# Two units of products on unscaled x, with the inverse root applied behind them, and x in eight column pieces

## The reference

```python
def _hybrid_layer(h, norm_w, w_in, ...):
    u = _rmsnorm(h, norm_w)                 # h * rsqrt(mean(h*h) + 1e-6) * norm_w
    proj = jnp.matmul(u, w_in)              # 2048 -> 22576 columns, then split
    (ml_q, ml_k, ml_v, ml_o, ml_z, ml_i, ml_f,
     dn_qkv, dn_z, dn_b, dn_a, gate_a, gate_b) = jnp.split(proj, idx, axis=-1)
    i_pre = _softcap(ml_i + ml_i_bias)
    logf  = log_sigmoid(_softcap(ml_f + ml_f_bias))
    qkv = _causal_conv_silu(dn_qkv, dn_conv_w)          # 4 taps over time
    ...
    beta = sigmoid(dn_b)
    g = -exp(dn_a_log) * softplus(dn_a + dn_dt_bias)
```

## Time and profile before

| | us |
|---|---|
| runs | 1913.67, 1914.96, 1916.21; median 1914.96 |
| span of the profiled execution | 1913.3 |
| TensorE, VectorE, ScalarE, POOL busy | 1895.3, 1398.8, 947.8, 344.2 |

### The profile page before, as it was taken

The page is one execution under the profiler, slowest core; times in us unless marked ns, Lnnn a source line. Parts: engine busy times, 40 slices in busy tenths (PEclk is TensorE's granted clock), DMA queues, the critical chain, the costliest instruction groups (busy, mean ns, idle before and its releaser), DMA issues.

```text
span 1913.3 us, 27611 instructions
## 1 busy us (share of the span) xinstructions
PE 1895.3 (99%) x10948; PEld 1638.9 (86%) x10948; DVE 1398.8 (73%) x1970; ACT 947.8 (50%) x1409; POOL 344.2 (18%) x543
## 2 busy tenths in 40 slices
PE   8999999999999999999999999999999999999998
PEld 8989999878888999988888888888888888888886
DVE  5686777676989888989989768665465686657675
ACT  6556566654544333444445465554444455544544
POOL 1025344351122222223223200000000000111000
PEclk9999999999999999999999999999999999999999
DMA  7455454555788877777888857755556543544563
GB/s 257 133 167 176 122 172 137 155 160 172 262 274 286 271 257 239 238 261 241 298 284 300 305 200 231 230 181 184 191 173 209 176 131 123 182 151 149 181 229 132
DMA packets 209744, 393.16 MB, mean 205 GB/s; under 512 B 13000, under 2 KB 62448, under 8 KB 208208
## 3 DMA queue, kind: packets, MB, share of 16 engines
q1 hardware_dynamic: 191248, 323.17, 51.6%
q0 software_dynamic: 18224, 68.17, 11.3%
q10 hardware_dynamic: 144, 0.07, 0.0%
HBM read 387.13 MB, written 4.23 MB: 205 GB/s over the span
## 4 chain that ended last, share of the span: by engine, by line
PE 94%; DVE 2%; ACT 2%; issue 1%; DMA 0%; SPq 0%; DVEq 0%; ACTq 0%
PE GB L2152 53%; PE GB L2179 18%; PE GB L2164 9%; PE GB L2167 5%; PE SB L415 1%; PE SB L1723 1%; PE SB L1715 1%; PE SB L819 1%; PE SB L784 1%; PE SB L1822 1%; PE SB L1829 1%; PE SB L1179 1%; ACT WH L2071 1%; DVE WL L2076 0%; DMA xin<-in_x 0%
## 5 line engine op out<-in xcount | busy, mean ns | idle before, releaser
L2076 DVE TENSOR_TENSOR WL<-raw,WH 128x1024 fp32r<-128x1024 f32 x605 | 732.3, 1237 | 197.4 <-ACT WH L2071 196.4
L2071 ACT ACTIVATE WH<-raw 128x1024 fp32r<-128x1024 f32 x605 | 621.7, 1057 | 320.5 <-PE GB L2152 227.1
L2152 PE MATMUL GB<-WH,uHL 128*128 128x512 f32 x1792 | 484.9, 392 | 0.0
L2152 PEld LDWEIGHTS GB<-WH,uHL 128*128 128x128 f32 x1792 | 333.3, 188 | 68.1 <-issue 0.5
L2179 PE MATMUL GB<-uHL,WH 128*128 128x256 f32 x2048 | 294.9, 287 | 1.6 <-DVE uHL L451 1.6
L2152 PE MATMUL GB<-WH,hHL 128*128 128x512 f32 x1024 | 279.5, 395 | 0.0
L2152 PE MATMUL GB<-WL,uHL 128*128 128x512 f32 x896 | 276.0, 389 | 0.0
L2179 PEld LDWEIGHTS GB<-uHL,WH 128*128 128x128 f32 x2048 | 265.6, 192 | 6.2 <-issue 3.4
L2152 PEld LDWEIGHTS GB<-WH,hHL 128*128 128x128 f32 x1024 | 190.6, 188 | 41.1 <-issue 2.7
L1409 DVE SCALAR_TENSOR_TENSOR macc<-wm,csil,macc 128x512 f32<-128x512 f32 x300 | 209.3, 745 | 2.8 <-DMA wm<-in_w_mod 1.7
L2152 PEld LDWEIGHTS GB<-WL,uHL 128*128 128x128 f32 x896 | 168.2, 188 | 35.4
(11 more groups left out here) (403 smaller groups left out, 1968.3 us busy)
## 6 DMA issues: line engine op xcount, KB each, us to landing
raw<-in_w_in SPq DMA_DIRECT2D x512, 512.0 KB, 4.6
raw<-in_w_out SPq DMA_DIRECT2D x96, 512.0 KB, 5.0
wm<-in_w_mod POOLq DMA_DIRECT2D x64, 512.0 KB, 5.5
wm<-in_w_mod POOLq DMA_DIRECT2D x64, 256.0 KB, 4.2
xin<-in_x SPq DMA_DIRECT2D x4, 512.0 KB, 5.7
E<-decay_rows POOLq DMA_DIRECT2D x4, 512.0 KB, 4.2
hres<-in_x POOLq DMA_DIRECT2D x1, 2048.0 KB, 10.8
cin<-in_ctx POOLq DMA_DIRECT2D x1, 2048.0 KB, 11.3
```

What stands on the lines that cost most here:

```text
L2071: e.activation(place(s)[0][:, :, :], raw[s % NR][:, :, :], ACT.Copy).then_inc(*wh.inc("WH", s))
L2076: e.tensor_tensor(low[:, :, :], raw[s % NR][:, :, :], f32(high[:, :, :]), sub).then_inc(*wl.inc("WL", s))
L2152: m = e.matmul(banks[j][:, :], x[:, c, 128 * j:128 * j + 128], w[:, k, :], start=i == 0 and k == 0 and n == 0, stop=i == 7 and k == 1 and ...
```

## The change

x now comes in eight column pieces (256 columns, all 256 tokens) that SP issues between the first weight slots (`FIRST_X`), `vcol` on ScalarE's queue. x is transposed and split without the inverse root, so uH and uL hold norm_w * x. Slot 0's products are ordered anew (`first_pe`), so that they begin with the high parts only. The squares of x are spread over slots 2 to 5 ("nxa"), root and Newton step over slots 5 and 6 ("nxd"). The root, one number for each token, is brought into a row on all partitions, `rrow`: two diagonal matrices times ones on TensorE, in the middle of slot 7 ("nxp").

Units 0 and 1 (RAW = 2) and the gates are computed on the unscaled x and multiplied by `rrow` behind: VectorE writes z = product * row to SBUF (`squares[1]`), and ScalarE's first tap and VectorE's taps read it there; the gates' products get the same (step "w"). From slot 9 on the activations themselves are rescaled, two k-blocks at a time: POOL adds uH + uL and multiplies by the row, ScalarE writes the new uH, VectorE the new uL ("rsp", "rsa", "rsd"); slot 16 + i waits for part i.

```diff
+RAW = 2
+NXA, NXD, NXP = (2, 3, 4, 5, 6, 7), (5.5, 6), (6.5,)
+FIRST_CONVS = (1, 1.5, 2, 3, 4, 5, 6, 10, 12, 13, 16)
...
+    for i in range(8):
+        at("rsp", 9 + i, (0,))
+        at("rsa", 11 + i, (0,))
+        at("rsd", 11 + i, (0.5,))
...
-            e.wait_ge(*g_pe.at("g"))
-            e.activation(rw[:, TT, :], SB[0][:, 0:256], ACT.Tanh, scale=1.0 / 15.0, bias=rb[:, 0:1]).then_inc(*g_act.inc("t"))
+            e.wait_ge(*g_dve.at("w"))
+            e.activation(rw[:, TT, :], rw[:, WW, :], ACT.Tanh, scale=1.0 / 15.0, bias=rb[:, 0:1]).then_inc(*g_act.inc("t"))
...
             yield
+            e.wait_ge(*g_pe.at("g"))
+            e.wait_ge(*nx_act.at("row"))
+            e.tensor_tensor(r(WW), SB[0][:, 0:256], rrow[:, :], mul).then_inc(*g_dve.inc("w"))
...
+        def norm_pe(e, bank):
+            e.wait_ge(*nx_dve.at("diag"))
+            claim(e, bank, 2, nx_act.at("row"))
+            m = e.matmul(SB[2][:, 0:256], ones[:, :], junk[:, 0:256], start=True, stop=True, skip_group_check=True)
+            m.then_inc(*nx_pe.inc("row"))
+            yield
...
         def busy_pe(e):
-            for said, n in ((init.at("ones"), 15), ((x_in[2], 16), 5), ((x_in[3], 16), 6), (nx_dve.at("ss"), 4)):
+            e.wait_ge(*init.at("ones"))
+            for _ in range(15):
...
+        def rescale_pool(e):
+            row = rrow[:, :].unsqueeze(1).to_broadcast([128, 2, 256])
+            for i in range(8):
+                k, scr = slice(2 * i, 2 * i + 2), halves_of[i % 2]
+                e.wait_ge(*slot.at("mm", 8 * RAW - 8 + i))
+                if i >= 2:
+                    e.wait_ge(*rs_dve.at("l", i - 2))
+                e.tensor_tensor(scr, f32(uH[:, k, :]), f32(uL[:, k, :]), add).then_inc(*rs_pool.inc("s", i))
+                if i == 0:
+                    e.wait_ge(*nx_act.at("row"))
+                e.wait_ge(*rs_pool.at("s", i))
+                e.tensor_tensor(scr, scr, row, mul).then_inc(*rs_pool.inc("r", i))
+                yield
+
+        def rescale_act(e):
+            for i in range(8):
+                e.wait_ge(*rs_pool.at("r", i))
+                e.activation(uH[:, 2 * i:2 * i + 2, :], halves_of[i % 2], ACT.Copy).then_inc(*rs_act.inc("h", i))
+                yield
+
+        def rescale_dve(e):
+            for i in range(8):
+                k = slice(2 * i, 2 * i + 2)
+                e.wait_ge(*rs_act.at("h", i))
+                e.tensor_tensor(uL[:, k, :], halves_of[i % 2], f32(uH[:, k, :]), sub).then_inc(*rs_dve.inc("l", i))
+                yield
...
+            if r < RAW:
+                e.wait_ge(*slot.at("mm", end("qkv", r)))
+                e.wait_ge(*nx_act.at("row"))
+                for j in range(4):
+                    v = e.tensor_tensor(squares[1][:, j, :], half(banks[j // 2], j % 2), rrow[:, :], mul)
+                v.then_inc(*z_dve.inc("z", r))
+                yield
...
-                    e.scalar_tensor_tensor(out=y[:, j, sh:], in0=half(banks[j // 2], j % 2)[:, 0:256 - sh],
+                    p = squares[1][:, j, :] if r < RAW else half(banks[j // 2], j % 2)
+                    e.scalar_tensor_tensor(out=y[:, j, sh:], in0=p[:, 0:256 - sh],
...
+            if (unit.kind, unit.n) == ("qkv", RAW):
+                e.wait_ge(*rs_dve.at("l", i))
...
+        FIRST_X = {0: (0,), 1: (1, 2), 2: (3,), 3: (4, 5), 4: (6, 7)}
...
             for s in range(NS):
+                for p in FIRST_X.get(s, ()):
+                    e.dma_start(xin[:, :, 256 * p:256 * p + 256],
+                                x_rows[:, :, 256 * p:256 * p + 256]).then_inc(x_in[p], 16)
...
         # ScalarE
-            norm_act(e)
-            split_act(e, 0)
-            e.wait_ge(*nx_dve.at("rstd"))
-            scaled_act(e, "a")
-            scaled_act(e, "b")
+            e.dma_start(vcol[:, :], A["c_vcol"]).then_inc(vcol_in, 16)
...
-            take_turns(stages, -1)
+            next(stages["u"])
+            split_act(e, 0)
+            next(stages["u"])
```

## The result

The kernel after takes **1935.28 us** (1933.34 to 1936.99, 4 runs), the kernel before beside it 1914.93: a ratio of 1.0109 [1.0095, 1.0124], +20.3 us. The direction of the forecast was right, its size was not: +12.5 was expected, and the time lies above the range (1912 to 1931).

What follows compares the result with a forecast made beforehand. TensorE, 99% busy, was taken to bound the kernel, its chain running through its products. Terms: -6.1 + 1.1 + 0.4 + 9.1 + 7 + 1 = +12.5 us on 1914.96, so 1927.5; range 1912 to 1931.

Steps and rivals of the forecast that it cites:

- the wait for the row: Slot 7: TensorE waits 1.1 us for the inverse root before the row product.
- VectorE's queue as walked: Slots 8 to 24: operations timed in queue order from the gates' products' end; low part WL16 ready 19.9 us after it.
- (a): Slots 8 to 24: VectorE late, POOL's products in its holes, the 7 us fall away; +5.5, 1920.5 us; chance 0.20.
- (b): Slots 8 to 24: VectorE catches up, so the 4.6 us head start stays; 1910.4 us; chance 0.12.
- (c): Slots 8 to 24: half of the lateness, 1911.5 to 1918.5 us, about no change; chance 0.13.
- (d): Start: pieces land later or clock stays low, first product gains only 2 us; +16.6, 1931.5 us; chance 0.07.
- head start: Behind slot 8: 6.1 us earlier first product less 1.1 wait and 0.4 row product leaves 4.6 us.
- POOL's constants ... nothing: Start: constants issued once slot 2 has landed, near 11 instead of 14 us, needed at slot 7; cost nothing.
- The term for contention: Rescaling: POOL's products and VectorE take turns; 7 us, from 12 products less five in holes; bounds 0 to 13.
- The term for lateness without contention: Slots 16 to 24: TensorE waits for VectorE's low parts, 6.6 + 0.7 + 1.8, together 9.1 us.
- The forecast's sum of waits: Slots 16 to 24: TensorE's waits on WL, the run's largest idle, 12 to 17 us in all.
- Behind slot 24: After slot 24: VectorE late at the gates' columns, 1 us more (0 to 1.5), then groups stand as before.

Runs made afterwards that it cites:

- e1b_pool_small: Kernel after with GpSimd's sum and product of the rescaling cut to 4 of 256 tokens per pair of chunks; 1925.41 us, ratio 1.0057.
- e5_const_late: Kernel after with GpSimd's constants issued only once slot 5's weights have landed, instead of slot 2's; 1931.65 us, ratio 1.0092.
- e9_psum2: Kernel after with gates' multiplication two slots later, constants behind slot 5's weights, and z multiplied in place in PSUM; 1924.24 us, ratio 1.0053.
- the start alone: Kernel after without multiplications by the row and rescaling (inverse root missing), constants behind slot 5's weights; 1909.36 us, ratio 0.9973 to the kernel before.
- e3_fillers: Kernel after with small matmuls on ones queued before TensorE's waits at slots 16, 17, 19, 20 and 24; 1934.76 us, ratio 1.0111.
- e11_psum7: Like e9_psum2, but seven units on unscaled activations, rescaling in slots 49 to 59, GpSimd's normalization moved earlier; 1917.26 us, ratio 1.0018.
- e12_psum7_order: Like e11_psum7, but GpSimd's key normalization ahead of the third pair's products, ScalarE's and VectorE's rescaling parts one slot later; 1919.26 us, ratio 1.0026.

## Why the prediction was wrong

**What held.** The first product (9.45, forecast 9.5); the wait for the row (1.05, forecast 1.1); VectorE's queue as walked. Without contention (e1b_pool_small, G = 49.9) WL16 is ready at 69.70, G + 19.8, forecast G + 19.9; WL20 at 87.30, G + 37.4, forecast 38.5; WL23 at 98.51, G + 48.6, forecast 49.6. The places of the waits, slots 16 to 24, and the mechanism beside GpSimd are as the trace shows them. Rival (a), GpSimd in VectorE's holes, is ruled out by e1b_pool_small, (b) and (c) by the waits on WL, and (d) by the first product at 9.45; that the head start still came out near (d)'s 2 us has another cause, the next one.

**The step that failed first: "POOL's constants ... nothing".** I asked when the constants are needed and not what lands behind them, though each weight slot was by then read 6 us earlier. They were 1.0 MB on top of weights that already kept the DMA engines at some 370 GB/s, and cost the start 4.0 us (e5_const_late); 1.5 of these are slot 4's lower clock behind the wait. My landing times ended at slot 4's; the one that bound was slot 5's, whose high part stands in ScalarE's queue ahead of the fifth pair. Two smaller errors: slot 0 ran at the full clock, 3.14 us, and not at 4.63 as I had kept it (1.5 gained), and the row product took 0.70, not 0.43 (0.3 lost). Together: head start 2.0 instead of 4.6, **2.6 us** of the error.

**The term for contention: 9.8 instead of 7** (within its bounds of 0 to 13), **2.8 us**. I let five of twelve products fall into holes and counted WL, the low parts and the taps as the operations that collide. Of the eight rows up to 91 us, four are steps of the gates (L575, L586, L595, L597: 4.2 of 9.3 us), which weren't on my list. The rule of the Trainium skill that I weighed ("SBUF — State Buffer", section "SBUF: two separate sides") covers them if they have two inputs in SBUF (L595, L597) or run in VectorE's two-port mode. The trace agrees with the lock for the whole instruction (1.27 for an operation of 0.17), and in e9_psum2 no tap is stretched once an operand is in PSUM; in which mode L575 and L586, with one input each, ran, it doesn't show.

**The term for lateness without contention: 12.0 instead of 9.1**, **2.9 us**. The walk ended with WL24 at G + 54.2. It came at 105.39, G + 55.5, since the taps before it took 3.66 instead of 1.43 beside GpSimd's own normalization (L860), which isn't of the rescaling and for which the sum had nothing. And slots 24 to 26 ran behind a wait at the lower clock, 10.24 us instead of 8.64, where I had priced the waits alone. The forecast's sum of waits, 12 to 17, was met (14.3), and the loss was still 21.8: a wait sum isn't a lateness when the slots behind the waits run slower. By its own terms the walk's last step is 1.7 and not 1.8, and ScalarE's 3.05 in the start is 3.03; neither matters.

**Behind slot 24**: 0.3 instead of 1 us; the 1.5 us wait near 126 is still 1.4. With these, 2.6 + 2.8 + 2.9 - 0.7 = 7.6 of the 7.8 us between +12.5 and +20.3.

Open is how the rescaling's 16.2 us divide beyond GpSimd's 9.8: eight low parts of 0.68 are 5.4, but no run had them alone. Nor is it settled what in the kernels with seven units takes the 8 to 10 us against the start alone: part goes before the rescaling begins, as above, and part beside it, and the waits and the slower matmuls behind them are what is seen of it.

## What to carry to other kernels

When an edit makes the first consumer start earlier, draw up again the landing of every transfer in flight, those "for later" too: here 1.0 MB of constants in flight beside slot 5's weights cost 4.0 of a possible 6.0 us. Where the forecast walks a queue, read from it when each result is ready and set TensorE's slots against that, with the clock behind the last wait in the sum. And GpSimd at work over SBUF beside a VectorE that is 88% busy (58 to 108 us) is not free time: price each of its products as one held VectorE operation, or let VectorE read PSUM.

## What the runs showed of the hardware

Short VectorE operations are hit as hard as long ones: 128x32 from 0.17 to 1.27 us. Multiplying by the row within PSUM costs what it costs into SBUF (415 and 412 ns for 128x256), so keeping z there costs VectorE nothing more. TensorE's clock stayed at the full level (2.4 GHz) behind a wait of 1.50 us before the first product, in front of which stood 6 us of matmuls on ones and the transposes of two pairs. Behind the wait of 2.35 us before slot 16 eight products still took 1.19 us; behind the next, 1.75 us long, they took 1.79, and behind those of 3.48 and 4.18 us 2.04 and 2.05, with a granted clock of 0.67 over 88 to 98 us, so most of that window at 1.2 GHz. The same wait doesn't always have the same sequel: behind slot 4's wait of 2.12 us the slot took 4.39 in after, behind one of 1.96 in e3_fillers 3.14; and behind a wait of 2.95 us before the same scores the first two matmuls took 2.05 in e11_psum7 and 1.10 in e12_psum7_order.
